# The end of a two-layer decoder trunk: a list of the expert blocks beyond capacity, and residual tiles kept for the last stage

## The reference

```python
weights = g_p * e_p / jnp.sum(e_p, axis=-1, keepdims=True)      # two experts of each token
expert_ids = g_idx * EXPERTS_PER_GROUP + e_idx
...
def expert_block(args):
    xb, e = args
    return (jax.nn.silu(xb @ w_gate[e]) * (xb @ w_up[e])) @ w_down[e]
...
y = jax.ops.segment_sum(y_buf[dest] * sw[:, None].astype(y_buf.dtype), st, num_segments=T)
...
h = h + y                                 # residual
out = rms_norm(h, final_norm)[:, N_META:]
```

## Time and profile before

| | us |
|---|---|
| median of 3 runs | 3834.31 (3830.76 to 3834.51) |
| profiled execution | 3818.64 |
| its span, first to last instruction | 3816.9 |
| TensorE busy in the span | 3369.3 (88%) |
| VectorE, ScalarE, GpSimd busy | 1779.6, 1306.1, 1718.7 |
| data moved by DMA | 540.12 MB, mean 142 GB/s |

### The profile page before, as it was taken

How to read it: one execution, slowest core, us unless ns; L and a number is a source line. 1 busy time by engine, 2 the same in 40 slices (tenths; PEclk the granted TensorE clock), 3 DMA queues, 4 the chain that set the end, 5 groups by cost and what they waited for, 6 DMA issues and landing times. The chain is left out here.

```text
span 3816.9 us, 60235 instructions
## 1 busy us (share of the span) xinstructions
PE 3369.3 (88%) x20523; PEld 2533.7 (66%) x20524; DVE 1779.6 (47%) x3671; ACT 1306.1 (34%) x2734; POOL 1718.7 (45%) x1345
## 2 busy tenths in 40 slices
PE   7999998897899996995999999999997978999920
PEld 5777775686788885994555555555556867888810
DVE  3554554576333335663555455445425653333306
ACT  3444444222232223443344344344342222222201
POOL 2232221243344432444877877887771223444302
PEclk9999999898899998996999999999998988999965
DMA  2001001643998857985011011101005439988519
GB/s 93 30 31 36 25 31 38 186 147 104 343 315 304 307 180 229 268 234 128 9 50 50 6 50 50 35 24 50 7 9 180 153 106 333 317 308 298 192 51 352
DMA packets 370812, 540.12 MB, mean 142 GB/s; under 512 B 94879, under 2 KB 291535, under 8 KB 363328
## 3 DMA queue, kind: packets, MB, share of 16 engines
q1 hardware_dynamic: 343584, 461.28, 38.3%
q0 software_dynamic: 27040, 76.40, 5.1%
HBM read 399.22 MB, written 146.96 MB: 143 GB/s over the span
## 5 line engine op out<-in xcount | busy, mean ns | idle before, releaser
L1959 POOL TENSOR_TENSOR ab_acc<-ab_acc,ab_pT 128x1024 f32<-128x1024 f32 (+2 forms) x320 | 654.1, 2044 | 187.1 <-ACT ab_pT L1994 158.9
L1994 ACT ACTIVATE ab_pT<-ab_S 128x512 f32<-128x512 f32 (+2 forms) x720 | 382.3, 532 | 644.4 <-PE ab_S L2074 374.8
L2006 DVE TENSOR_REDUCE ab_mx<-ab_W 128x2 f32<-128x800 f32 (+4 forms) x360 | 350.4, 977 | 459.5 <-PE ab_W L2089 273.5
L2134 PE MATMUL ab_O<-ab_pT,ab_v 128*64 128x512 f32 (+4 forms) x1408 | 338.0, 558 | 0.0
L2072 PE MATMUL ab_S<-ab_q_hi,ab_k_hi 97*128 97x512 f32 (+2 forms) x720 | 310.1, 431 | 1.4 <-DVE ab_q_hi L2019 1.4
L2072 PEld LDWEIGHTS ab_S<-ab_q_hi,ab_k_hi 97*128 97x128 f32 x720 | 137.5, 191 | 257.1 <-ACT ab_pT L1994 134.8
L1324 PE MATMUL ex_G<-ex_xT,ex_wg 128*128 128x160 f32 x2048 | 295.3, 303 | 5.8 <-DMA ex_wu<-in_moe_w_up 5.8
L1324 PEld LDWEIGHTS ex_G<-ex_xT,ex_wg 128*128 128x128 f32 x2048 | 284.5, 192 | 10.2 <-DMA ex_wu<-in_moe_w_up 6.6
L1324 PE MATMUL ex_U<-ex_xT,ex_wu 128*128 128x160 f32 x2048 | 288.6, 299 | 0.0
L1198 POOL DMA_INDIRECT scratch_y<-ex_y,ex_prow x64 | 64.8, 1012 | 490.2 <-issue 360.4
L1324 PEld LDWEIGHTS ex_U<-ex_xT,ex_wu 128*128 128x128 f32 x2048 | 281.7, 190 | 0.0
(11 more groups left out here) (293 smaller groups left out, 7066.5 us busy)
## 6 DMA issues: line engine op xcount, KB each, us to landing
ex_wg<-in_moe_w_gate SPq DMA_DIRECT2D x64, 1024.0 KB
ex_wu<-in_moe_w_up SPq DMA_DIRECT2D x64, 1024.0 KB
ex_wd<-in_moe_w_down SPq DMA_DIRECT2D x64, 1024.0 KB
pr_o<-scratch_oT SPq DMA_DIRECT2D x34, 512.0 KB
scratch_h<-pr_h SPq DMA_DIRECT2D x34, 512.0 KB
scratch_xn<-pr_xn SPq DMA_DIRECT2D x34, 512.0 KB, 2.7
pb_y<-scratch_y SPq DMA_DIRECT2D x17, 1024.0 KB
fi_y<-scratch_y SPq DMA_DIRECT2D x16, 1024.0 KB, 8.1
```

The lines of the kernel that those rows point to most:

```text
L1959: nc.gpsimd.tensor_tensor(to, to, pT[0:r, U % RING, :, 0:n], ALU.add).then_inc(added, 1)
L1994: nc.scalar.activation(pT[0:r, U % RING, h, 0:n], S[0:r, h, 0:n], ACT.Exp, scale=B_SCALE).then_inc(exped, 1)
L2006: nc.vector.reduce_max(mx[:, :, t, c:c + 1].rearrange("p h a -> p (h a)"), W[:, j % 2, :, 0:n], AX.X).then_inc(emptied, 1)
L2134: last = nc.tensor.matmul(O[HD * h:HD * h + HD, G % 2, 512 - n:512], v[0:r, p % 2, h, b, :], pT[0:r, U % RING, h, 0:n], start=(U == opens[ ...
```

## The change

Four edits at the end of the kernel and in the experts of both layers.

- `experts`: VectorE makes a list of the blocks beyond capacity, in ten pieces `list_beyond(1)` to `list_beyond(10)` at its steps 1 to 10, behind `find_places` and ahead of the product h, with small tiles in one partition. For this its steps up to 11 are written out (its loop begins at 12), and SP loads one more constant, `index`.
- `experts` of layer 1: SP loads ten tiles of the residual `h` into `keep["h"]`, at its steps 2 to 5 and then once in each turn of its loop, between the up weights and the down weights.
- `experts_beyond`: the search through counts is replaced by one loop over the 32 entries of the list, with one comparison for each; expert and start are loaded only for an entry that is there.
- `finish`: written out without loops. `y` has eight buffers and is loaded eight tiles ahead, the six remaining residual tiles are loaded after the first eight `y` tiles, `xn` has four buffers, and the order of the sums and scales on VectorE stays.

```diff
+EARLY = 10
+BEYOND = 2 * KEYS // P
@@ experts, SP
                 sp.dma_start(quarter[:, :], io["quarter"]).then_inc(consts, 16)
+                sp.dma_start(index[:, :], io["iota"][0:1, :]).then_inc(consts, 16)
@@
+                    if layer == 1 and (e.c in (2, 3, 4, 5) if e.turn is None else e.c == 6):
+                        t = (e.c + 4) if e.turn is None else e.turn
+                        at = slice(t, t + 1) if e.turn is None else bass.ds(t, 1)
+                        sp.dma_start(keep["h"][:, at, :].rearrange("p a d -> p (a d)"),
+                                     dram["h"][P:ROWS, :].rearrange("(t p) d -> t p d", p=P)[at, :, :].rearrange("a p d -> (a p) d")
+                                     ).then_inc(keep["h_in"], 16)
@@ experts, VectorE
+                def list_beyond(k):
+                    counts, listed = keep["counts"][0:1, 0:EXPERTS], keep["extra"]
+                    if k == 1:
+                        nc.vector.tensor_scalar(limit[:, :], index[:, 0:OVER], float(P), float(CAP), ALU.mult, ALU.add)
+                        dve.drain()
+                        nc.vector.tensor_tensor(grid[:, :, 0:OVER], along(counts, EXPERTS, OVER), across(limit[:, :], EXPERTS, OVER), ALU.is_gt)
+                    if k == 2:
+                        nc.vector.reduce_sum(blocks[:, :], grid[:, :, 0:OVER], AX.X)
+                    if k == 3:
+                        nc.vector.tensor_tensor(grid[:, :, :], along(index[:, :], EXPERTS, EXPERTS), across(index[:, :], EXPERTS, EXPERTS), ALU.is_ge)
+                    if k == 4:
+                        nc.vector.tensor_tensor(grid[:, :, :], grid[:, :, :], across(blocks[:, :], EXPERTS, EXPERTS), ALU.mult)
+                    if k == 5:
+                        nc.vector.reduce_sum(upto[:, :], grid[:, :, :], AX.X)
+                    if k == 6:
+                        nc.vector.tensor_copy(listed[0:1, 0:1], upto[:, EXPERTS - 1:EXPERTS])
+                        nc.vector.tensor_tensor(grid[:, :, :], along(index[:, :], BEYOND, EXPERTS), across(upto[:, :], BEYOND, EXPERTS), ALU.is_ge)
+                    if k == 7:
+                        nc.vector.reduce_sum(whose[:, :], grid[:, :, :], AX.X)
+                    if k == 8:
+                        nc.vector.tensor_tensor(grid[:, :, :], grid[:, :, :], across(blocks[:, :], BEYOND, EXPERTS), ALU.mult)
+                    if k == 9:
+                        nc.vector.reduce_sum(ahead[:, :], grid[:, :, :], AX.X)
+                        nc.vector.tensor_scalar(whose[:, :], whose[:, :], float(EXPERTS - 1), None, ALU.min)
+                    if k == 10:
+                        nc.vector.tensor_tensor(ahead[:, :], index[:, 0:BEYOND], ahead[:, :], ALU.subtract)
+                        nc.vector.tensor_copy(listed[0:1, 1:1 + BEYOND], whose[:, :])
+                        nc.vector.tensor_scalar(first[:, :], whose[:, :], float(STRIDE), float(CAP), ALU.mult, ALU.add)
+                        dve.drain()
+                        nc.vector.scalar_tensor_tensor(out=listed[0:1, 1 + BEYOND:1 + 2 * BEYOND], in0=ahead[:, :], scalar=float(P), in1=first[:, :],
+                                                       op0=ALU.mult, op1=ALU.add)
+                    dve.drain()
@@
                         find_places(e.back(-1))
+                    if e.turn is None and 1 <= e.c <= 10:
+                        list_beyond(e.c)
@@
-                over_steps(dve, 0, 2 + EXPERTS, 4, EXPERTS - 4, step, unroll=4)
+                over_steps(dve, 0, 2 + EXPERTS, 12, EXPERTS - 4, step, unroll=4)
@@ experts_beyond
-    with nc.If(count(slice(EXPERTS, EXPERTS + 1)) > 0):
-        with nc.Fori(0, EXPERTS) as e:
-            n = count(bass.ds(e, 1))
-            with nc.If(n > CAP):
-                with nc.Fori(0, OVER) as b:
-                    with nc.If(n > b * P + CAP):
-                        expert_block(nc, io, dram, layer, e, e * STRIDE + b * P + CAP)
+    n = entry(slice(0, 1), BEYOND)
+    with nc.If(n > 0):
+        with nc.Fori(0, BEYOND) as i:
+            with nc.If(n > i):
+                e = entry(bass.ds(i + 1, 1), EXPERTS - 1)
+                start = entry(bass.ds(i + (1 + BEYOND), 1), EXPERTS * STRIDE)
+                expert_block(nc, io, dram, layer, e, start)
@@ finish, SP
+                for t in range(DEEP):
+                    load(t)
+                for t in range(EARLY, NB):
+                    sp.dma_start(h[:, t - EARLY, :], dram["h"][P * (t + 1):P * (t + 2), :]).then_inc(h_in, 16)
+                for t in range(NB):
+                    sp.wait_ge(xn_ready, t + 1)
+                    if t + DEEP < NB:
+                        load(t + DEEP)
+                    sp.dma_start(out[P * t:P * t + P, :], xn[:, t % 4, :]).then_inc(xn_out[t % 4], 16)
@@ finish, VectorE
+                def scale(t):
+                    dve.wait_ge(rstd_ready, t + 1)
+                    if t >= 4:
+                        dve.wait_ge(xn_out[t % 4], 16 * (t // 4))
...
+                for t in range(NB + 1):
+                    if t < NB:
+                        combine(t)
+                    if t >= 1:
+                        scale(t - 1)
```

More of the change, by code:

```diff
@@ L46 @@
 TC = [(0, P), (P, CAP - P)]
+EARLY = 10
+BEYOND = 2 * KEYS // P
+assert CAP > P and BEYOND == EXPERTS
 class At:
@@ L1088, in experts @@
         quarter = s.sb("quarter", [P, 1])
+        index = s.sb("index", [1, EXPERTS])
+        limit = s.sb("limit", [1, OVER])
+        grid = s.sb("grid", [1, EXPERTS, EXPERTS])
+        blocks = s.sb("blocks", [1, EXPERTS])
+        upto = s.sb("upto", [1, EXPERTS])
+        whose = s.sb("whose", [1, BEYOND])
+        ahead = s.sb("ahead", [1, BEYOND])
+        first = s.sb("first", [1, BEYOND])
         wg = s.sb("wg", [P, 4, DC, FE])
@@ L2285, in _, with load @@
                 sp.dma_start(gain[:, :], bcast(io["final_norm"], D)).then_inc(consts, 16)
[L2287 to L2306, removed]
+                def load(t):
+                    sp.dma_start(y[:, t % DEEP, :, :].rearrange("p k d -> p (k d)"),
+                                 dram["y"].rearrange("(r k) d -> r (k d)", k=2)[P * (t + 1):P * (t + 2), :]).then_inc(y_in[t % DEEP], 16)
+                for t in range(DEEP):
[7 more added lines that the diff above has]
+                    sp.dma_start(out[P * t:P * t + P, :], xn[:, t % 4, :]).then_inc(xn_out[t % 4], 16)
+                for b in range(4):
+                    sp.wait_ge(xn_out[b], 16 * (NB // 4))
             @block.gpsimd
@@ L2311, in _ @@
                 pool.drain()
[L2313 to L2316, removed]
+                for t in range(NB):
+                    r = rstd[:, t:t + 1]
+                    pool.wait_ge(squared, t + 1)
+                    nc.gpsimd.tensor_scalar(r, ssq[:, t:t + 1], 1.0 / D, EPS, ALU.mult, ALU.add)
@@ L2317, in step @@
                     pool.drain()
-                    nc.gpsimd.tensor_tensor(rstd[:, i.slot:i.slot + 1], rstd[:, i.slot:i.slot + 1], half[:, :], ALU.pow).then_inc(rstd_ready, 1)
-                over_steps(pool, 0, NB, 4, NB, step, unroll=4)
+                    nc.gpsimd.tensor_tensor(r, r, half[:, :], ALU.pow).then_inc(rstd_ready, 1)
             @block.scalar
             def _(act):
-                def step(i):
-                    act.wait_ge(summed, i.count(1, 1))
-                    nc.scalar.activation(hsq[:, :], h[:, i.slot4, :], ACT.Square, accum_out=ssq[:, i.slot:i.slot + 1])
+                for t in range(NB):
+                    act.wait_ge(summed, t + 1)
+                    nc.scalar.activation(hsq[:, :], residual(t), ACT.Square, accum_out=ssq[:, t:t + 1])
@@ L2326, in step @@
                     act.drain().then_inc(squared, 1)
-                over_steps(act, 0, NB, 4, NB, step, unroll=4)
             @block.vector
             def _(dve):
-                dve.wait_ge(consts, 16)
[L2333 to L2351, removed]
@@ L2352, in _, with combine @@
-                over_steps(dve, 0, 1 + NB, 4, NB, step, unroll=4)
+                def combine(t):
+                    if t == 0:
+                        dve.wait_ge(keep["h_in"], 16 * EARLY)
+                    if t == EARLY:
+                        dve.wait_ge(h_in, 16 * (NB - EARLY))
+                    dve.wait_ge(y_in[t % DEEP], 16 * (t // DEEP + 1))
+                    for k in range(2):
+                        nc.vector.scalar_tensor_tensor(out=residual(t), in0=y[:, t % DEEP, k, :], scalar=keep["weights"][:, t + 1, k:k + 1],
+                                                       in1=residual(t), op0=ALU.mult, op1=ALU.add)
+                        dve.drain()
+                    dve.sem_inc(summed, 1)
```

39 lines of the change are left out of this document (25 added, 14 removed).

## The result

The changed kernel took 3784.5 us in the median of four runs (3781.9 to 3789.0), the kernel before 3834.4 (3830.8 to 3844.6): ratio 0.9867, 95% interval 0.9845 to 0.9888, so 51 us less (43 to 59). The profiled execution of the changed kernel had a span of 3780.8 us, 36.1 less than that of before. The forecast was 3795 us with a range of 3784 to 3812; the gain came out larger than forecast, 51 instead of 39 us.

The account below looks back on a forecast made before the run. Taken as bounds: TensorE in layer 1's experts, almost nothing busy during the search, transfers in the last stage. The terms -27.2 - 0.4 - 12.2 + 0 + 0 + 0.9 = -38.9 took 3834.3 to 3795 us, range 3784 to 3812.

Parts of the forecast that it names:

- Search in front of the block: Search for blocks beyond capacity, layer 1: 2.7 us before the block instead of 29.9, so the block begins 27.2 us earlier.
- Search behind it: After the found block: 31 refused entries at 0.48 us, 14.9 against 15.3 us, so 0.4 us less.
- Early tiles: Ten h tiles loaded in the experts of layer 1: cost 0, covered by the queue's lead; bounds 0 and 12.5 us.
- List: List of blocks on VectorE in the experts: 23.2 us of work in both layers, cost 0; bounds 0 and 23.2.
- Rival 5: Experts: list pieces delay TensorE and its clock falls, twenty steps x 3.7 = 73 us, net 3869; chance 0.04.
- Constants: One more DMA issue of 0.43 us on SP ahead of the first slots in both layers: 0.9 us more.
- Last stage, the start and the stall: First y lands at 7.1 us, store 0 is done at 36.4, VectorE waits 5 to 7 us for it at scale 4.
- Last stage, the steady part: After the stall: one y load and one store per 4.33 us, a store tile at 1.84 us; stage ends at 86.4.
- Last stage, the size of before: The old last stage taken as 98.6 us from the profile, against 86.4 for the new: gain 12.2 us.
- From profile to median: Timed median 3834.3, 15.7 us above the profiled execution, outside anything the change touches; gain subtracted from the median.
- Rival 1: Last stage: all bytes move at 350 GB/s, end at 93.4 us, gain there 5.2, total 3802; chance 0.12.
- Rival 2: Last stage: stores pass loads in the queue, no stall at scale 4, stage 77.0 us, gain 21.6, total 3786; chance 0.10.

Follow-up runs that it names:

- the second comparison: The changed kernel, unchanged, timed again against the kernel before: ratio 0.9884 (0.9867 to 0.9901).
- the second profile: The kernel before, unchanged, run and profiled again: span 3830.6 us, last stage 108.6 us, ratio 1.000 to itself.
- no_early: The changed kernel with all sixteen h tiles loaded in the last stage, none in the experts: ratio 0.9903 to the kernel before, last stage 95.8 us.
- new_y4: The changed kernel with four buffers for y instead of eight: ratio 0.9860 to the kernel before, last stage 79.3 us.
- old_xn4: The kernel before with four buffers for xn and nothing else changed: ratio 0.9964 to the kernel before, last stage 90.1 us.
- list_x4: The changed kernel with three more 1024-element operations in each of list pieces 4 to 10: ratio 0.9928 to the kernel before.
- early_x4: The changed kernel with three DRAM-to-DRAM copies issued beside each of the ten early h tiles: ratio 0.9892 to the kernel before.

## Why the prediction was right and where it was wrong

- *Search in front of the block*: 2.7 us forecast, 2.6 measured; gain 27.3 instead of 27.2. Right, in its mechanism and in its size.
- *Search behind it*: 0.4 us less forecast, none measured (49.1 and 49.2 us between the two starts). A comparison with i was taken at 0.48 us and costs 0.50, nearly the 0.51 to 0.52 of the one that it replaces.
- *Early tiles*: nothing forecast, and the experts took 491.2 and 491.9 us against 491.7 and 492.7. One detail was wrong: SP's issue of a tile wasn't 0.43 us but 3.3 in the median (1.2 to 7.0); it had that time. The kernel with three copies beside each tile shows the cover's end, 0.32 us a copy. They also took 5.2 MB out of the last stage, and more than their bytes: without them the one wait for store 0 was 17.1 us and not 6.7.
- *List*: nothing forecast, nothing seen. Its longest operation took 1.21 us in one partition, close to the 1.28 taken from 128. Rival 5, a stall with a falling clock, didn't come at the list's own size: the granted clock was 1.00 from 3190 to 3350 us. With four times as much in seven steps it came once.
- *Constants*: 0.9 us more forecast, nothing seen. The issue is there (0.32 us), but the experts took 491.3 and 491.2 us in the two layers against 490.7 and 491.7.
- *Last stage, the start and the stall*: first sum at 7.1 us forecast, 7.3 measured; store 0 at 36.4 and 35.7; stall 5 to 7 and 6.7. Right.
- *Last stage, the steady part*: here a term was mis-sized. The prediction took 5.58 us a tile in the old stage, subtracted 3.74 for the loads and gave the remaining 1.84 to the store tile. A store tile has half a MiB like an h tile and costs the same 1.25 when enough is queued (426 GB/s over the pairs). The 0.6 us between were not the price of the bytes but came with the two xn buffers: a scale waits for the store before last, and the next load waits for the scale. So the pairs weren't 4.33 us but at most 3.74, VectorE's 4.03 took over at once, and the stage ended at 83.4 instead of 86.4. Of these 3.0 us, 2.1 are the seven pairs; the rest is the stall, which ended 0.7 us earlier, and the tail.
- *Last stage, the size of before*: the step that failed most. The prediction took 98.6 us from one execution as if it were the stage's length. It was the shortest of three that were profiled (98.6, 104.8, 108.6). The gain of this stage is 15 to 25 us, and the 12.2 lie below all of it: 3.0 us are missing from the new stage, and 0 to 10 from the old one. With the mean of the three (104.0) the second part is 5.4 us. So of the 12 us between the gain forecast and the one measured, 3.0 lie in the new stage, about 5 in the old one, 0.9 in the constants and -0.4 behind the block; some 3 are left, less than the interval of 43 to 59 us tells apart (the second comparison has 44).
- *From profile to median*: "15.7 above that execution, outside of anything the change touches". This was asserted and not read from a row, and it was wrong: in the second profile 10.0 of 13.7 us lay in the last stage. The sum took 98.6 us from one execution and subtracted the gain from the median of others.

Rival 1 had its rows for it: 350 GB/s as a mean and 381 with stores. Both were signs of the closed loop and not of a limit of the transfers. The Trainium skill's figure of 358 GB/s for the HBM side ("DMA: Bandwidth & Descriptors", section "Where 436 GB/s comes from") isn't what bound here: that section gets it by dividing a stack's 716 GB/s by two cores, one core ran here, and in no_early 423 to 427 GB/s were kept up over 60 us, first without stores and then with them. Rival 2 (stores pass the loads) didn't come in the changed kernel, and did when they were given a queue of their own.

What stays open: why a stage with little queued shows DMA engines busy at 0.94 to 1.02 of the time and yet moves 314 to 381 GB/s. The 360 GB/s at a share of 1.01 in new_y4, with four buffers and VectorE as the bound, show that it isn't peculiar to two store buffers: a share near 1 doesn't prove that the transfers are at their limit. The records count a packet as busy from start to end, so the packets themselves took longer; no run here tells on what they waited, nor why one execution fell to 381 and another to 314.

## What to carry to other kernels

A transfer's price taken by subtraction from a loop that waits for its own stores is the price of the loop; look for the wait that ends each turn before calling the rest bandwidth, and try one more pair of buffers there first (old_xn4: a few words in eight lines, 14 us, interval 9 to 19). Deep buffers in front of a queue in order have a cost of their own: whatever is queued first stands ahead of the first store, so load as many as the consumer uses until that store can go, and no more. And a stage's length from one execution is a sample: where it will be subtracted from, look at a second one.

## What the hardware showed that was not expected

- The same last stage ran at 381, about 330 and 314 to 349 GB/s in three executions of the same code with two store buffers, and with four at 419 to 422 in old_xn4 and 423 to 427 in no_early as long as the transfers were the bound.
- Loads and stores together run as fast as loads alone: 424 to 427 GB/s in both.
- An issue on SP costs 0.33 to 0.43 us with little outstanding. With much outstanding it took up to 7.0 us (an early h tile), and six h tiles took 11.3 us behind 8 MB of y and 3.1 us behind 4 MB.
- TensorE's clock fell to the lower level after a wait of 4.3 us in a stretch that was otherwise full (list_x4), and again after two waits of 3.4 and 2.9 us, 17 us apart (early_x4); it was back about 6 and 4 us later.
- A refused entry costs 0.50 us on SP whatever is compared, with two gaps of 0.12 to 0.13 us behind its branches in each turn, and TensorE's branches take 0.22 us; a search over 31 empty entries is 15 us of an otherwise idle chip.
